# Gate slot first, zero matmuls behind norm sums, and expert slots divided by row blocks, in a three-layer block with experts

## The reference

```
h = modulated_norm(x, norm_g[l, 0], sh1, sc1)             # rmsnorm(x, g) * (1 + scale) + shift
x = x + 0.5 * g1 * swiglu(h, ffn_wg[l, 0], ffn_wu[l, 0], ffn_wd[l, 0])
h = modulated_norm(x, norm_g[l, 1], sh2, sc2)
x = x + g2 * m                                            # m: attention and pooling (l = 0), short convolution (l = 1)
h = modulated_norm(x, norm_g[l, 2], sh3, sc3)
x = x + 0.5 * g3 * swiglu(h, ffn_wg[l, 1], ffn_wu[l, 1], ffn_wd[l, 1])
...
# third block, last part: each token goes to one of 4 groups and to 2 of its 8 experts
(jax.nn.silu(xb @ w_g[e]) * (xb @ w_u[e])) @ w_d[e]       # w_g, w_u: 1024 x 256, w_d: 256 x 1024
```

## Time and profile before

| | |
|---|---|
| median of 3 runs | 1726.16 us (1724.48 to 1728.0) |
| the profiled execution | 1724.32 us, span 1722.5 us |
| TensorE's granted clock, mean | 0.955 of full speed |
| loads | 379.90 MB |
| expert stage | from about 1394 us to about 1698 us of the span |

### The profile page before, as it was taken

How to read it: one execution, slowest core, us unless ns; L and a number is a source line. 1 busy time by engine, 2 the same in 40 slices (tenths; PEclk the granted TensorE clock), 3 DMA queues, 4 the chain that set the end, 5 groups by cost and what they waited for, 6 DMA issues and landing times.

```text
span 1722.5 us, 29138 instructions
## 1 busy us (share of the span) xinstructions
PE 1609.0 (93%) x12267; PEld 1522.4 (88%) x12267; DVE 1130.3 (66%) x1156; ACT 780.7 (45%) x808; POOL 17.2 (1%) x24
## 2 busy tenths in 40 slices
PE   5999989789999999998988999899899889999995
PEld 3999988579999999998988999898788689999994
DVE  2777777567777677756645454664664568888983
ACT  2433344434333443334434333444454447777772
POOL 0000000300000000000000000000000000000000
PEclk8999999889999999999998999999999889999997
DMA  9897766336878587863625555354332518898980
GB/s 323 273 329 278 271 242 242 125 123 248 289 270 313 173 292 270 313 196 126 196 98 171 177 188 177 126 171 117 110 123 98 218 54 347 342 357 346 357 327 26
DMA packets 202482, 379.90 MB, mean 221 GB/s; under 512 B 12185, under 2 KB 157470, under 8 KB 190110
## 3 DMA queue, kind: packets, MB, share of 16 engines
q1 hardware_dynamic: 202398, 378.70, 62.4%
HBM read 377.63 MB, written 1.05 MB: 220 GB/s over the span
## 4 chain that ended last, share of the span: by engine, by line
PE 84%; DVE 7%; ACT 4%; DMA 3%; issue 1%; SPq 0%; ACTq 0%; DVEq 0%
PE ps L579 20%; PE ps L580 19%; PE ps L581 19%; PE ps L1183 3%; PE ps L1185 3%; PE ps L1184 3%; DVE wlo L1678 3%; ACT whi L1300 2%; PE ps L1208 2%; PE ps L1209 2%; PE ps L1210 2%; DMA ada_raw<-in_w_ada_dram 2%; PE ps L690 2%; DVE rstd L1744 1%; PE ps L705 1%
## 5 line engine op out<-in xcount | busy, mean ns | idle before, releaser
L1678 DVE TENSOR_TENSOR wlo<-raw,whi 128x2048 fp32r<-128x2048 f32 (+1 forms) x191 | 432.9, 2267 | 346.5 <-ACT whi L1300 346.4
L579 PE MATMUL ps<-hhi,whi 128*128 128x256 f32 (+1 forms) x2024 | 587.7, 290 | 27.8 <-DVE hlo L1688 16.7
L580 PE MATMUL ps<-hlo,whi 128*128 128x256 f32 (+1 forms) x2024 | 579.1, 286 | 0.0
L581 PE MATMUL ps<-hhi,wlo 128*128 128x256 f32 (+1 forms) x2024 | 578.7, 286 | 0.0
L1300 ACT ACTIVATE whi<-raw 128x2048 fp32r<-128x2048 f32 (+1 forms) x191 | 360.1, 1886 | 209.9 <-PE ps L581 164.2
L579 PEld LDWEIGHTS ps<-hhi,whi 128*128 128x128 f32 (+1 forms) x2024 | 395.1, 195 | 35.8 <-issue 26.5
L580 PEld LDWEIGHTS ps<-hlo,whi 128*128 128x128 f32 (+1 forms) x2024 | 395.1, 195 | 1.8 <-issue 1.4
L581 PEld LDWEIGHTS ps<-hhi,wlo 128*128 128x128 f32 (+1 forms) x2024 | 394.8, 195 | 0.0
L579 PE MATMUL ps<-hidhi,whi 128*128 128x256 f32 x704 | 201.0, 286 | 2.8 <-DVE wlo L1805 2.8
L581 PE MATMUL ps<-hidhi,wlo 128*128 128x256 f32 x704 | 199.2, 283 | 0.0
L580 PE MATMUL ps<-hidlo,whi 128*128 128x256 f32 x704 | 199.2, 283 | 0.0
(11 more groups left out here) (276 smaller groups left out, 2449.7 us busy)
## 6 DMA issues: line engine op xcount, KB each, us to landing
ada_raw<-in_w_ada_dram SPq DMA_DIRECT2D x72, 1024.0 KB, 5.3
raw<-in_ffn_wg_dram SPq DMA_DIRECT2D x44, 1024.0 KB, 5.6
raw<-in_ffn_wu_dram SPq DMA_DIRECT2D x44, 1024.0 KB, 5.4
raw<-in_ffn_wd_dram SPq DMA_DIRECT2D x44, 1024.0 KB, 6.8
raw<-in_w_in_dram SPq DMA_DIRECT2D x18, 1024.0 KB, 5.4
raw<-in_w_exp_gate_dram SPq DMA_DIRECT2D x16, 1024.0 KB, 6.6
raw<-in_w_exp_up_dram SPq DMA_DIRECT2D x16, 1024.0 KB, 8.6
raw<-in_w_exp_down_dram SPq DMA_DIRECT2D x16, 1024.0 KB, 4.8
```

What stands on the lines that cost most here:

```text
L579: pe.matmul(o, wh, xh, start=start, stop=False, skip_group_check=shared)
L580: pe.matmul(o, wh, xl, start=False, stop=False, skip_group_check=shared)
L581: return pe.matmul(o, wl, xh, start=False, stop=stop, skip_group_check=shared)
L1678: dve.tensor_tensor(wlo[s][:, 0:width], raw[s][:, 0:width], whi[s][:, 0:width].bitcast(F32), ALU.subtract).then_inc(split[s], 1)
```

## The change

1. `first_two` takes only slot 0 for each tile (both halves of its output features), gives it back, and then waits for slot 1 and does its product.
2. `norm_sums` can be followed by 18 or 30 matmuls of zeros on bank 6 (`keep_clock`): in mix0, ffn1, ffn2, mix1, ffn3 and blk2, not in ffn0 and not ahead of the router and at the end. They wait for bank 6 and for the modulation vectors.
3. For ffn3's first chunk the load of up is issued ahead of that of gate.
4. The experts' raw buffers of gate and up lie side by side. Slot 0 takes rows 0 to 3 of 8 of both matrices, slot 1 rows 4 to 7 of both. A matmul then has gate's and up's 256 columns as one moving operand of 512. ScalarE's copy for slot 0 waits for both loads; SyncE's load of gate waits for slot 1's split, that of up for none.

```diff
-        raw = [sb(f"raw{s}", [P, UW]) for s in range(3)]
+        raw_all = sb("raw", [P, 3, UW])
+        raw = [raw_all[:, s, :] for s in range(3)]
...
+        def expert_part(s, parity):
+            if s == 2:
+                return weights_of(s, parity)
+            both = ada_raw[:, :, :] if parity else raw_all[:, 0:2, :]
+            return both[:, :, s * UW // 2:(s + 1) * UW // 2]
+        def as_part(s, t):
+            return t[:, :] if s == 2 else t[:, :].rearrange("p (w n) -> p w n", w=2)
...
-                    load(0, c + b[0], wg(c))
-                    load(1, c + b[1], wu(c))
+                    for s in ((1, 0) if stage == "ffn3" and isinstance(c, int) and c == 0 else (0, 1)):
+                        load(s, c + b[s], (wg, wu)[s](c))
...
-                    if not isinstance(e, int) or e > 1:
-                        sp.wait_ge(split[s], e + (b_moe[s] - 1))
+                    if s != 1 and (not isinstance(e, int) or e > 1):
+                        last_reader = split[max(s, 1)]
+                        sp.wait_ge(last_reader, e + (b_moe[max(s, 1)] - 1))
...
-            def first_two():
-                def product(s, k, m):
+            def first_two(second):
+                def product(s, k, m, start):
                     c = slice(k * 2 * P + m * P, k * 2 * P + (m + 1) * P)
                     return three(ps[:, s, m * T:(m + 1) * T], whi[s][:, c], wlo[s][:, c], hhi[:, k, :], hlo[:, k, :],
-                                 k == 0, k == KT - 1)
+                                 start, k == KT - 1, shared=True)
                 for k in range(KT):
                     wait("h_ready")
-                    for s in range(2):
-                        product(s, k, 0)
-                for s in range(2):
+                    for m in range(2):
+                        mm = product(0, k, m, k == 0 and m == 0)
+                mm.then_inc(used[0], 1)
+                second()
+                for m in range(2):
                     for k in range(KT):
-                        mm = product(s, k, 1)
-                    mm.then_inc(used[s], 1)
+                        mm = product(1, k, m, k == 0)
+                mm.then_inc(used[1], 1)
             def first_units(freed_by):
-                for s in range(2):
-                    slot_ready(s)
-                    own(s)
-                first_two()
+                slot_ready(0)
+                own(0)
+                first_two(second=lambda: (slot_ready(1), own(1)))
...
-            def norm_sums():
+            def keep_clock(n, vectors):
+                if n:
+                    own(6)
+                    pe.wait_ge(sem("mod_ready"), vectors)
+                for _ in range(n):
+                    pe.matmul(ps[:, 6, T:2 * T], zeros[:, :], zeros[:, :].rearrange("p (o n) -> p o n", o=1).to_broadcast([P, 2, P]),
+                              start=True, stop=True)
+            def norm_sums(fill=0, vectors=0):
...
                 frees(7, "stat_read")
+                keep_clock(fill, vectors)
...
-                pe.wait_ge(split[1], b0[1] + 1)
-                if ch:
-                    pe.wait_ge(sem("hid_done"), ch)
-                first_two()
+                def second():
+                    pe.wait_ge(split[1], b0[1] + 1)
+                    if ch:
+                        pe.wait_ge(sem("hid_done"), ch)
+                first_two(second)
...
-            norm_sums()
+            norm_sums(30, 7)
             first_units(("sq_done", "sq_done"))
...
-            norm_sums()
+            norm_sums(18, 9)
             chunked("ffn1", 9)
-            norm_sums()
+            norm_sums(18, 14)
             chunked("ffn2", 14, 4)
...
-                o = ps[:, p, s * CH:(s + 1) * CH]
-                for k in range(KT):
-                    if isinstance(e, int) and e == 0 and s == 0:
+                o = ps[:, p, :]
+                wh, wl = (w[s][:, :].rearrange("p (w k n) -> p k w n", w=2, k=KT // 2) for w in (whi, wlo))
+                for j in range(KT // 2):
+                    k = KT // 2 * s + j
+                    if isinstance(e, int) and e == 0:
                         wait("gathered_split")
-                    c = slice(k * CH, (k + 1) * CH)
-                    pe.matmul(o, hi[:, k, :], whi[s][:, c], start=(k == 0), stop=False)
-                    pe.matmul(o, hi[:, k, :], wlo[s][:, c], start=False, stop=False)
-                    mm = pe.matmul(o, lo[:, k, :], whi[s][:, c], start=False, stop=(k == KT - 1))
+                    pe.matmul(o, hi[:, k, :], wh[:, j], start=(k == 0), stop=False, skip_group_check=True)
+                    pe.matmul(o, hi[:, k, :], wl[:, j], start=False, stop=False, skip_group_check=True)
+                    mm = pe.matmul(o, lo[:, k, :], wh[:, j], start=False, stop=(k == KT - 1), skip_group_check=True)
...
+            def expert_high(s, e, p):
+                for part in ((0, 1) if s == 0 else (s,)):
+                    if p:
+                        act.wait_ge(landed_odd[part], e * 8 + 8)
+                    else:
+                        act.wait_ge(landed[part], e * 8 + (b_moe[part] + 1) * 16)
+                act.wait_ge(used[s], e + b_moe[s])
+                copy(as_part(s, whi[s]), expert_part(s, p)).then_inc(high[s], 1)
...
-                if n < len(widths[s]):
+                if n == b_moe[s]:
+                    expert_high(s, 0, 0)
+                    turn[s] += 1
+                elif n < len(widths[s]):
...
-            def expert_high(s, e, p):
-                if p:
-                    act.wait_ge(landed_odd[s], e * 8 + 8)
-                else:
-                    act.wait_ge(landed[s], e * 8 + (b_moe[s] + 1) * 16)
-                act.wait_ge(used[s], e + b_moe[s])
-                copy(whi[s][:, :], weights_of(s, p)).then_inc(high[s], 1)
...
+            def expert_low(s, e, p):
+                dve.wait_ge(high[s], e + (b_moe[s] + 1))
+                dve.tensor_tensor(as_part(s, wlo[s]), expert_part(s, p), as_part(s, whi[s]).bitcast(F32),
+                                  ALU.subtract).then_inc(split[s], 1)
```

More of the change, by code:

```diff
@@ L962, in outputs @@
                     linear(stage, u0 + j, "x_ready", mhi, mlo, ready if j == 0 else None)
-            norm_sums()
+            norm_sums(18, 9)
             chunked("ffn1", 9)
-            norm_sums()
+            norm_sums(18, 14)
             chunked("ffn2", 14, 4)
-            norm_sums()
+            norm_sums(30, 18)
             first_units(("evacuated", "v_done"))
@@ L974, in _ @@
             outputs("mix1", 12, lambda k: wait("mix_split") if k % 2 == 0 else None)
-            norm_sums()
+            norm_sums(18, 18)
             chunked("ffn3")
-            norm_sums()
+            norm_sums(30, 18)
             def rope(r):
@@ L1300, in split_high, with copy @@
                 act.activation(whi[s][:, 0:width], raw[s][:, 0:width], ACT.Copy).then_inc(high[s], 1)
+            def copy(o, i, scale=1.0):
+                return act.activation(o, i, ACT.Copy, scale=scale)
+            def expert_high(s, e, p):
[6 more added lines that the diff above has]
+                copy(as_part(s, whi[s]), expert_part(s, p)).then_inc(high[s], 1)
             def refill(s):
                 n = turn[s]
-                if n < len(widths[s]):
+                if n == b_moe[s]:
+                    expert_high(s, 0, 0)
+                    turn[s] += 1
+                elif n < len(widths[s]):
                     split_high(s, n, widths[s][n])
                     turn[s] += 1
-            def copy(o, i, scale=1.0):
-                return act.activation(o, i, ACT.Copy, scale=scale)
             def norm(slots=()):
@@ L1679, in split_low @@
                                   ALU.subtract).then_inc(split[s], 1)
+            def expert_low(s, e, p):
+                dve.wait_ge(high[s], e + (b_moe[s] + 1))
+                dve.tensor_tensor(as_part(s, wlo[s]), expert_part(s, p), as_part(s, whi[s]).bitcast(F32),
+                                  ALU.subtract).then_inc(split[s], 1)
             def refill(s):
                 n = turn[s]
-                if n < len(widths[s]):
+                if n == b_moe[s]:
+                    expert_low(s, 0, 0)
+                    turn[s] += 1
+                elif n < len(widths[s]):
                     split_low(s, n, widths[s][n])
@@ L2208, in _ @@
             dve.tensor_tensor(hot1, hot1, hot2, ALU.add).then_inc(sem("slot_weights"), 1)
-            def expert_low(s, e, p):
-                dve.wait_ge(high[s], e + (b_moe[s] + 1))
-                dve.tensor_tensor(wlo[s][:, :], weights_of(s, p), whi[s][:, :].bitcast(F32), ALU.subtract).then_inc(split[s], 1)
             def expert_hidden(e, p):
```

## The result

The changed kernel takes 1733.96 us (median of 7 runs, 1731.88 to 1738.17). The kernel before took 1725.37 us in the 7 runs beside them. The ratio is 1.006, 95% interval 1.0038 to 1.0083: slower by 0.4 to 0.8%. The forecast was 1734.7 us. The profiled execution took 1731.88 us, 7.6 above that of before. Its page first, to be held against the earlier trace rows: TensorE is as busy as before, and its clock is a little higher.

A forecast was written before the change was run, and what follows sets the result against it. TensorE was taken to bound the kernel before. 27 us lost in the experts less 18.5 gained gave +8.5: 1732.8 us on the profiled execution, 1734.7 on the median; the forecast's own range was 1725 to 1745.

The forecast's parts named there:

- part 4 of the sum: Expert stage: row blocks in the slots make the first copy wait for up's load too; 27 us lost, bounds 19 to 33.
- The ring of the prediction: Expert stage: batch issued, up landed, first copy, splits and hidden product, next batch; 19.5 us for two experts.
- the prediction's last sentence: Experts: forecast would be wrong if up's landing time shrank with the slower pace, or half clock appeared; no size given.
- The straight ring: Expert stage: the loop from batch to batch with nothing added on top; 18.94 us for two experts in one traced round.
- the lower bound that was given: Expert stage: both kinds of batch at the even ones' landing; loop 18.9 us for two experts, loss 19 us.
- part 3: Expert stage: two matmuls of 256 columns become one of 512; 0.26 us per expert, 8.3 us in 32, if TensorE stays the bound.
- parts 1 and 2: Norms and ffn3's first loads: gate slot first, zeros behind the sums, up loaded before gate; 18.5 us gained together.
- If the zeros did not hold the clock, only the slot order would be left: Norms: without the clock held, four stops of 1.6 us, the swap's 1.7 and about a microsecond remain; some 9 us gained.
- The load swap: ffn3's first loads, up before gate: the twelve earlier sums run on into the last four; 1.7 us gained.
- B: Rival, expert stage: up's landing does not bind, TensorE stays the bound; 18.5 + 8.3 gained, 1699.4 us; chance 0.12.
- C: Rival, norms: expert loop as forecast, but zeros don't hold the clock or delay the products; +18, 1744 us; chance 0.15.
- D: Rival, expert stage: the loop's waits lower TensorE's clock, 0.5 to 1 us more per pair; +10, 1745 us; chance 0.13.

The follow-up runs named there:

- Order: The changed kernel with gate and up of each expert loaded ahead of down of the expert before it; 1696.29 us, ratio 0.9842.
- gate third: The changed kernel with its old expert stage put back, but expert loads issued up, gate, down; 1735.08 us, ratio 1.0061.
- no swap: The changed kernel with ffn3's first loads in the order gate, up again; 1738.22 us, ratio 1.0095.
- rows only: The kernel before with the row blocks and the wide matmuls alone, norms and ffn3's loads as before; 1753.34 us, ratio 1.0153.
- no zeros: The changed kernel without the zero matmuls behind the norm sums; 1736.15 us, ratio 1.007.

## Why the prediction came out right, and where it didn't

**The experts (part 4 of the sum): mechanism right, two terms off, in opposite directions.** Forecast 27 us lost, measured 29.0, where kernels with this same stage spread over 6 us. The ring of the prediction is in the trace piece by piece: 9.1 us from first copy to batch (9.03 in the round shown), up third, VectorE's three splits behind it. *Order* and *gate third* show that the position of the load is the cause. But up's landing was put at 10.4 us behind the batch; it is (1.29 + 8.6 + 1.01 + 8.8) / 2 = 9.85. The 9.8 of odd experts in the earlier trace rows was measured where batches followed every 8.74 us, and at the slower pace it was 8.8, 1.0 less, as the prediction's last sentence warned (even experts' 8.6 stayed as it was; that the pace is the reason is likely, but was not tried alone). The straight ring is 18.95, the lower bound that was given, and 9.48 per expert instead of 9.75: over 29 steps 0.27 x 29 = 8 us less lost. The other term is what comes on top of the straight ring. The prediction took it as equal to before, as the work at the group ends, and it is 14.3 - 6.2 = 8 us more. Little of this stands at the group ends: the three steps at each of them hold all but 0.1 of the 6.2 before, and 4.8 of the 14.3 now. The three steps with half clock are the longest of all, and the clock's share is up to some 5 us by the estimate above; the rest stays open. The two errors cancel. The sum was right partly by luck.

**The wide matmuls (part 3)** were priced at 0.26 us per expert if TensorE is the bound; 0.29 measured.

**The norms (parts 1 and 2): sum right, shares wrong.** Forecast 18.5 us, measured 20.8. By stage, forecast and measured: ffn0 1.5 and 1.8; mix0 2.1 and 1.9; ffn1 3.1 and 2.9; ffn2 4.1 and 3.3; mix1 with ffn3 5.9 and 6.4; blk2 1.8 and 4.1. The same code took 249.6 to 256.6 us for blk2 and 222.8 to 227.3 for ffn0 in different kernels here, so those two gains are not tied to the change. The step that failed is "If the zeros did not hold the clock, only the slot order would be left", with its "some 9 us" left of 18.5. Without the zeros the kernel lost 2.2 us by the medians and 3.6 over the five stages of the table, not 9.5. Two reasons can be read from the rows; neither was tried alone. The prediction took the 7 us at half clock of ffn2 for all norms, and half of them had 3.5. And with the gate slot first the clock stood at half for 3.5 us, partly under tiles that VectorE delivers late anyway. Slot order is worth 6.9 us by the medians and 6.4 by the stages (4.9 in the table's five, 1.5 in ffn0), mostly the four stops of 1.6 us. The load swap was put at 1.7; it is 4.3 by the medians, 3.1 by mix1's time: in *no swap* ScalarE's wait is 11.48 us, not 10.28, and TensorE stops for two squares, 2.6 us together, not for one. Undone one by one the parts make 2.2 + 6.9 + 4.3 = 13.4 of 20.8 by the medians, and 3.6 + 6.4 + 3.1 = 13.1 by the stages. The rest is ffn0's and blk2's own spread, and what either zeros or slot order does alone.

**The rivals.** B (up's landing does not bind) is excluded by the trace: up lands 9.85 us behind its batch, and B needed 7.9. *Order*, where up lands at 7.4, reaches 1696.3 us, near the 1699.4 that B had said: B's number was that of a kernel with another load order. C fell twice: the zeros held the clock, and their absence costs a quarter to two fifths of the price that C put on it (2.2 or 3.6 of 9.5). D is there in part: the clock falls three times in the stage, which costs up to some 5 us where D had 10. In the changed kernel TensorE stands still in two of three steps, for up to 2.9 us, and yet in the 35 us shown the clock stays at 1.00; over 200 us it is 0.98. The Trainium skill's pattern (the same page, HAM oscillation) of a low clock in each round is not what this trace shows, three falls in 31 steps; the loop that the page describes has longer waits, of about 3 to 5 us. The first of the three falls came with the longest wait, 2.88 us, but the third with one of 2.26:

```profile
1416.50 0.79 PE L1211 MATMUL ps<-whi,hhi 128*128 128x512 f32 x1 [2.88 <-DVE wlo L1716]
```

## What to carry to other kernels

When a change alters which data an engine needs first, write down the order in which the loads leave and land beside the order of use: here the same matmuls cost 29 us or gained 9, by nothing but the place of one load among three. Close each chain of waits into a ring and compare its length with the busiest engine's time; an engine at 100% can have a ring about 1% shorter behind it (17.3 beside 17.5 us here, by the prediction's working). And do not carry a landing time over to another pace: it belongs to the spacing of the batches in which it was measured.

## What was not expected of the hardware

- Three 1 MB loads issued within 1.3 us land at +4.9, +7.4 and +9.9 us, at 425 GB/s in the stretch shown. Halving the first took 0.25 us on the mean off the third, and the stream then ran at 387 GB/s.
- Behind the six norms a spell at half clock was mostly 3.5 or 6.7 us, ahead of ffn3 also 8.6 (rows only) and 10.2 (the kernel before). The gap does not tell which of them: before, the gap of 4.09 us gave 6.7 in mix0 and 3.5 in mix1, the one of 2.36 us 3.5 in ffn1 and 6.7 in ffn2. The same gap of 2.42 us ahead of ffn3 made one in four kernels of ten.
- An idle of 2.36 us in ffn2 gave a first matmul of 0.55 us in one kernel and of 0.36 us in another (no zeros), where the clock fell only afterwards.
- In the expert stage the length of a wait does not tell whether the clock falls: 2.26 us brought a fall, 2.39 us none.
